# Merge stage: gate and branch products by one level of Strassen's scheme, over halves of the tokens

## The reference

```
proj = h @ w_in                                  # its last 3*1024 columns are the gates
gA, gB, gC = split(sigmoid(gates), 3)
merged = gA * (yA_gated @ w_br_rwkv) + gB * (yB_gated @ w_br_mla) + gC * (yC_gated @ w_br_sb)
x = x + gate * (merged @ w_out)                  # w_out is 1024 x 1024
```

## Time and profile before

| | us |
|---|---|
| median of the runs | 5366.02 |
| profiled execution, first to last instruction | 5380.9 |
| PE busy | 4843.3 (90%) |
| DVE, ACT, POOL busy | 2057.0, 1544.8, 240.7 |
| products of the merge, layer 1 (window 2002 to 2562) | 560, PE busy 559.82 |
| output of the merge, layer 1 (window 2562 to 2690) | 128, PE busy 123.71 |

### The profile page before, as it was taken

The page is one execution under the profiler, slowest core; times in us unless marked ns, Lnnn a source line. Parts: engine busy times, 40 slices in busy tenths (PEclk is TensorE's granted clock), DMA queues, the critical chain, the costliest instruction groups (busy, mean ns, idle before and its releaser), DMA issues. The chain is left out here.

```text
span 5380.9 us, 64260 instructions
## 1 busy us (share of the span) xinstructions
PE 4843.3 (90%) x24624; PEld 3178.1 (59%) x24624; DVE 2057.0 (38%) x4480; ACT 1544.8 (29%) x3518; POOL 240.7 (4%) x506
## 2 busy tenths in 40 slices
PE   6999898788989989999969898987889899899999
PEld 2667567456656655555426676674566566555554
DVE  2355555335534450111123555553355344501111
ACT  2333232235543340000023332322355433400000
POOL 0010100000000000000000101000000000000000
PEclk8999999899999989999979999998999999899999
DMA  5100101210012111211140101012100121112111
GB/s 199 23 12 19 30 9 17 78 48 10 24 43 69 61 54 36 72 59 41 59 155 23 12 19 30 9 17 78 48 10 24 45 69 59 54 36 73 58 41 59
DMA packets 132705, 253.24 MB, mean 47 GB/s; under 512 B 51445, under 2 KB 86517, under 8 KB 126919
## 3 DMA queue, kind: packets, MB, share of 16 engines
q1 hardware_dynamic: 132280, 244.32, 14.3%
q10 hardware_dynamic: 112, 4.72, 0.2%
HBM read 201.66 MB, written 52.06 MB: 47 GB/s over the span
## 5 line engine op out<-in xcount | busy, mean ns | idle before, releaser
L2376 PE MATMUL banks<-hT,w_gate 128*128 128x384 f32 x2304 | 771.4, 488 | 15.9 <-DMA w_branch<-in_w_br 15.9
L2376 PEld LDWEIGHTS banks<-hT,w_gate 128*128 128x128 f32 x2304 | 439.8, 191 | 323.9 <-DMA w_branch<-in_w_br 16.7
L974 PE MATMUL banks<-hT,w_piece 128*128 128x384 f32 x1536 | 564.1, 510 | 9.7 <-ACT raw L1078 9.4
L2143 PE MATMUL banks<-hT,w_piece 128*128 128x384 f32 x1152 | 391.1, 495 | 17.8 <-DMA w_piece<-in_w_cols 16.4
L974 PEld LDWEIGHTS banks<-hT,w_piece 128*128 128x128 f32 x1536 | 288.0, 199 | 186.9 <-issue 27.5
L2380 PE MATMUL banks<-y_branch,w_branch 128*128 128x384 f32 x1152 | 395.1, 486 | 0.0
L2401 ACT ACTIVATE gate_tanh<-banks 128x384 f32<-128x384 f32 x144 | 70.6, 490 | 1065.4 <-PE banks L2380 1065.4
L2143 PEld LDWEIGHTS banks<-hT,w_piece 128*128 128x128 f32 x1152 | 217.0, 193 | 173.8 <-issue 22.1
L2380 PEld LDWEIGHTS banks<-y_branch,w_branch 128*128 128x128 f32 x1152 | 218.9, 190 | 152.6
L2414 DVE SCALAR_TENSOR_TENSOR gate_tanh<-gate_tanh,banks 128x384 f32<-128x384 f32 x96 | 53.2, 554 | 634.1 <-ACT gate_tanh L2401 634.1
L2392 PE MATMUL banks<-w_out,mergedT 128*128 128x512 f32 x576 | 247.5, 592 | 0.0
(11 more groups left out here) (335 smaller groups left out, 8017.9 us busy)
## 6 DMA issues: line engine op xcount, KB each, us to landing
w_piece<-in_w_cols SPq DMA_DIRECT2D x68, 512.0 KB, 4.4
w_ada<-in_w_ada SPq DMA_DIRECT2D x12, 2048.0 KB, 9.5
w_gate<-in_w_cols SPq DMA_DIRECT2D x48, 512.0 KB, 3.4
y_branch<-y_gated SPq DMA_DIRECT2D x18, 768.0 KB, 9.6
w_branch<-in_w_br SPq DMA_DIRECT2D x48, 256.0 KB, 3.5
sb_cached_keysT<-in_sbkT SPq DMA_DIRECT2D x8, 1024.0 KB, 6.7
sb_cached_values<-in_sbv SPq DMA_DIRECT2D x8, 1024.0 KB, 5.1
w_out<-in_w_out SPq DMA_DIRECT2D x16, 512.0 KB, 5.1
```

The costliest lines, as they stand in the source:

```text
L974: last = mm(dst, w[0 if kind in ("k", "v") else 1][:, k, :], hT[:, k, c], start=(k == 0), stop=(k == KD - 1))
L2143: last = mm(ps[:, bank[n], 0:TG], w[wn % 3][:, k, :], hT[:, k, TG * g:TG * g + TG], start=(k == 0), stop=(k == KD - 1))
L2376: nc.tensor.matmul(ps[:, 2 * (u % 4), 0:TG], wg[j % 2][:, k, :], hT[:, k, c], start=(k == 0), stop=(k == KD - 1))
```

## The change

One level of Strassen's scheme, in the form with seven products, is put on both products of the merge. A unit is now (half of the tokens `tp`, branch `b`, pair of output blocks `m`): 2 x 3 x 4 = 24 units per layer. The weights of two output blocks are cut into 2 x 2 parts (output block x half of the contraction), and `hT` or `y_branch` into 2 x 2 parts (half of the contraction x quarter of the tokens, `TQ` = 288). Seven products of parts and of their sums take the place of eight. A product has 4 matmuls for the gate and 2 for the branch, with 288 columns.

The sums of weights (four instructions for the gate, four for the branch in each unit) and of `y_branch` (four for each branch and half of the tokens) are made by GpSimd, those of `hT` by VectorE. Products that several results share are copied out of PSUM by ScalarE (`kept`), and VectorE adds them up (`added`). All weights are loaded twice, once for each half of the tokens. `w_out` goes into `hT`'s space, and x moves in half rows.

The core of the diff (left out: declarations of tiles and semaphores, and the SyncE program, which loads 2 x 512 KB of `w_gate` and 2 x 256 KB of `w_branch` for unit u after product 7 and product 14 of unit u-2):

```diff
+        units = [(tp, b, m) for tp in range(2) for b in range(3) for m in range(KD // 2)]
         @block.gpsimd
+            def combine(w, s, half, sem):
+                a11, a12, a21, a22 = (w[:, i, half * j:half * j + half, :] for i in range(2) for j in range(2))
+                own(G.tensor_tensor(s[:, 0], a21, a22, ALU.add))
+                own(G.tensor_tensor(s[:, 1], s[:, 0], a11, ALU.subtract))
+                own(G.tensor_tensor(a21, a11, a21, ALU.subtract))
+                own(G.tensor_tensor(s[:, 2], a12, s[:, 1], ALU.subtract), sem)
+            for u in range(NU):
+                pool.wait_ge(wg_loaded[u % 2], 32 * (u // 2 + 1))
+                combine(wg[u % 2], wgs[u % 2], KD // 2, gate_sums)
+                if u % PER_Y == 0:
+                    ... four tensor_tensor of 128 x (2 x 288) on Y, then y_sums
+                pool.wait_ge(wb_loaded[u % 2], 32 * (u // 2 + 1))
+                combine(wb[u % 2], wbs[u % 2], HP // 2, branch_sums)
         @block.tensor
-                for k in range(KD):
-                    nc.tensor.matmul(ps[:, 2 * (u % 4), 0:TG], wg[j % 2][:, k, :], hT[:, k, c], ...)
-                for k in range(HP):
-                    last = nc.tensor.matmul(ps[:, 2 * (u % 4) + 1, 0:TG], wb[j % 2][:, k, :], Y[b % 2][:, k, c], ...)
+            def product(bank, w, b, first, last):
+                half = w.shape[1]
+                for k in range(half):
+                    ins = mm(ps[:, bank, 0:TQ], w[:, k, :], b[:, k, :], start=(first and k == 0), stop=(k == half - 1), skip_group_check=True)
+                ins.then_inc(products, 1)
+            for u, (tp, b, m) in enumerate(units):
+                pe.wait_ge(wg_loaded[u % 2], 32 * (u // 2 + 1))
+                if u >= 1:
+                    pe.wait_ge(tanh_done, 4 * u)
+                product(0, w[:, 0, 0:half], hT[:, 0:half, c1], True, False)
+                product(1, w[:, 0, half:KD], hT[:, half:KD, c1], True, True)
+                pe.wait_ge(gate_sums, u + 1)
+                pe.wait_ge(h_sums, tp + 1)
+                pe.wait_ge(kept, 6 * u + 1)
+                product(0, s[:, 1], HS[:, 1], False, False)
+                product(2, s[:, 0], HS[:, 0], True, False)
+                pe.wait_ge(kept, 6 * u + 2)
+                product(0, w[:, 1, 0:half], hT[:, 0:half, c2], False, False)
+                pe.wait_ge(kept, 6 * u + 3)
+                product(2, s[:, 2], hT[:, half:KD, c2], False, True)
+                pe.wait_ge(added, 6 * u + 2)
+                product(0, w[:, 1, half:KD], HS[:, 2], False, True)
+                ... the same seven for the branch: banks 3, 4, 5 for 0, 1, 2, wb and Y for wg and hT,
+                ... waits quarter_read u; branch_sums, y_sums, kept 6u+4; kept 6u+5; kept 6u+6; added 6u+5
         @block.scalar
-                nc.scalar.activation(th[u % 2][:, :], ps[:, 2 * (u % 4), 0:TG], ACT.Tanh, scale=0.5).then_inc(gate_read, 1)
+            for u in range(NU):
+                keep(u, 1, gk[:, 0, :], 0)
+                keep(u, 3, gk[:, 1, :], 0)
+                tanh(u, 0)
+                keep(u, 4, gk[:, 2, :], 2)
+                tanh(u, 1)
+                tanh(u, 2)
+                act.wait_ge(products, 14 * u + 7)
+                if u >= 1:
+                    act.wait_ge(quarter_read, u)
+                do(gq[:, 3, :], ps[:, 0, 0:TQ], ACT.Tanh, scale=0.5).then_inc(tanh_done, 1)
+                keep(u, 8, bk[:, 0, :], 3)
+                keep(u, 10, bk[:, 1, :], 3)
+                keep(u, 11, bk[:, 2, :], 5)
         @block.vector
+            h_sum(0)
+            for u, (tp, b, m) in enumerate(units):
+                add(u, 2, 1, gq[:, 0, :], gk[:, 0, :], 1)
+                add(u, 5, 3, gq[:, 1, :], gk[:, 2, :], 0)
+                add(u, 6, 2, gq[:, 2, :], gk[:, 1, :], 2)
+                if u == NU // 2 - 1:
+                    dve.wait_ge(products, 14 * u + 7)
+                    h_sum(1)
+                add(u, 9, 4, bq[:, 0, :], bk[:, 0, :], 4)
+                quarter(0, 0, 0, bq[:, 0, :])
+                add(u, 12, 6, bq[:, 1, :], bk[:, 2, :], 3)
+                add(u, 13, 5, bq[:, 2, :], bk[:, 1, :], 5)
+                quarter(1, 1, 1, bq[:, 1, :])
+                quarter(2, 0, 1, bq[:, 2, :])
+                quarter(3, 1, 0, ps[:, 3, 0:TQ], quarter_read)
```

More of the change, by code:

```diff
@@ L2356, in _ @@
[L2356 to L2363, removed]
@@ new lines, in _ @@
+            for j in range(4):
+                sp.dma_start(x[j][:, :], x_half(*ups[j])).then_inc(x_moved[j], 16)
+            sp.wait_ge(products, 14 * (NU - 1) + 7)
+            sp.dma_start(w_half(1), A["w_out"][l, :, :, 512:D]).then_inc(w_out_loaded[1], 16)
+            for j, (n, i) in enumerate(ups):
+                sp.wait_ge(updated, 2 * (j + 1))
+                sp.dma_start(x_half(n, i), x[j % 4][:, :]).then_inc(x_moved[j % 4], 16)
+                if j >= 1 and j + 3 < len(ups):
+                    sp.wait_ge(x_moved[(j - 1) % 4], 16 * (2 * ((j - 1) // 4) + 2))
+                    sp.dma_start(x[(j - 1) % 4][:, :], x_half(*ups[j + 3])).then_inc(x_moved[(j - 1) % 4], 16)
@@ new lines, in _ @@
+            banks = (6, 7, 0, 1)
+            pe.wait_ge(merged, NU // 2)
+            for j, (n, i) in enumerate(ups):
+                if i == 0:
+                    pe.wait_ge(w_out_loaded[n], 16)
+                if j == 2:
+                    pe.wait_ge(tanh_done, 4 * NU)
+                if j == 4:
+                    pe.wait_ge(merged, NU)
+                if j >= 4:
+                    pe.wait_ge(update_read, j - 3)
+                for k in range(KD):
+                    last = mm(ps[:, banks[j % 4], :], M[:, k, P * i:P * i + P], w_half(n)[:, k, :], start=(k == 0), stop=(k == KD - 1))
@@ L2396, in _, with keep @@
         def _(act):
[L2397 to L2400, removed]
-                nc.scalar.activation(th[u % 2][:, :], ps[:, 2 * (u % 4), 0:TG], ACT.Tanh, scale=0.5).then_inc(gate_read, 1)
+            do = nc.scalar.activation
+            def keep(u, j, dst, bank):
+                act.wait_ge(products, 14 * u + j)
+                do(dst, ps[:, bank, 0:TQ], ACT.Copy).then_inc(kept, 1)
@@ new lines, in add, with quarter @@
+            def add(u, j, copied, dst, src, bank):
+                dve.wait_ge(products, 14 * u + j)
+                dve.wait_ge(kept, 6 * u + copied)
+                own(V.tensor_tensor(dst, src, ps[:, bank, 0:TQ], ALU.add), added)
+            h_sum(0)
+            for u, (tp, b, m) in enumerate(units):
+                def quarter(q, row, col, src, sem=None):
+                    out = M[:, 2 * m + row, cols(tp, col)]
+                    if b == 0:
+                        own(V.scalar_tensor_tensor(out, gq[:, q, :], 1.0, src, ALU.add, ALU.mult), sem)
+                    else:
+                        own(V.scalar_tensor_tensor(gq[:, q, :], gq[:, q, :], 1.0, src, ALU.add, ALU.mult), sem)
+                        own(V.tensor_tensor(out, out, gq[:, q, :], ALU.add))
+                add(u, 2, 1, gq[:, 0, :], gk[:, 0, :], 1)
[5 more added lines that the diff above has]
+                add(u, 9, 4, bq[:, 0, :], bk[:, 0, :], 4)
+                dve.wait_ge(tanh_done, 4 * u + 1)
+                quarter(0, 0, 0, bq[:, 0, :])
+                add(u, 12, 6, bq[:, 1, :], bk[:, 2, :], 3)
+                add(u, 13, 5, bq[:, 2, :], bk[:, 1, :], 5)
+                dve.wait_ge(tanh_done, 4 * u + 3)
+                quarter(1, 1, 1, bq[:, 1, :])
+                quarter(2, 0, 1, bq[:, 2, :])
+                dve.wait_ge(products, 14 * u + 14)
+                dve.wait_ge(tanh_done, 4 * u + 4)
+                quarter(3, 1, 0, ps[:, 3, 0:TQ], quarter_read)
+                V.engine_nop().then_inc(merged, 1)
@@ L2406, in _ @@
             dve.wait_ge(gate_loaded, 16)
             own(V.tensor_scalar(gate[:, :, :], gate[:, :, :], 0.5, None, ALU.mult))
[L2408 to L2422, removed]
+            put = InOrder(dve, updated)
+            for j, (n, i) in enumerate(ups):
+                dve.wait_ge(updates, j + 1)
+                dve.wait_ge(x_moved[j % 4], 16 * (2 * (j // 4) + 1))
+                put(V.tensor_tensor(t[j % 2][:, :], ps[:, (6, 7, 0, 1)[j % 4], :], gate[:, int(i == NPT), 512 * n:512 * n + 512], ALU.mult))
```

154 lines of the change are left out of this document (101 added, 53 removed).

## The result

The changed kernel takes 5235.05 us (median of 4 runs, 5230.34 to 5236.68) against 5366.52 us for the kernel before: 0.9754 of its time, 95% interval 0.974 to 0.9768. Forecast: 5234, range 5222 to 5288.

What follows compares the result with a forecast made beforehand. TensorE was taken to bound the merge without a gap. Per layer -68.4 + 0.7 + 2.1 - 0.3 = -65.9 us, twice -131.8, took 5366.0 to 5234 us, range 5222 to 5288.

Steps and rivals of the forecast that it cites:

- The likeliest case: Whole kernel: the time comes out as reckoned, 5234 us, own range 5224 to 5262; chance 0.65.
- The stream: Merge products on TensorE: 2016 records of 288 columns at 242.5 ns take 488.9 us, 68.4 us less per layer.
- The narrow waits: Four branch waits per unit on ScalarE copies or VectorE adds: latency of 0.78 to 0.87 us fits in 0.97, cost 0.
- The sums on GpSimd: Weight and y sums: 232 us beside 489 us of TensorE per layer, one unit ahead, hidden behind matmuls, cost 0.
- the second rival: GpSimd slow beside VectorE: if twice as slow, TensorE waits at y sets, about 50 us in all, 5284 us; chance 0.09.
- `h_sum(1)`: VectorE's sums of hT in unit 11 after product 7: TensorE's product 14 stalls, +2.1 us per layer.
- the clock rival: Merge: more gaps lower TensorE's granted clock; half level for a fifth of the stream gives 5430 us; chance 0.03.
- The start: Each layer's first matmul waits for 1.0 MB of gate weights instead of 0.75 MB of both: +0.7 us.
- the output part: Products with w_out after the merge's products: records unchanged; the last store of 256 KB instead of 512 gives -0.3 us per layer.
- The product windows: Sign of being wrong: the merge's two product windows don't shrink to 490 to 495 us each.
- narrow waits don't fit: Each of four branch waits opens a gap of about 0.3 us, 1.2 us a unit, 58 in all: 5292 us; chance 0.17.
- Every product drains: Each of 14 products per unit pays 0.33 us for emptying TensorE's array, 222 us in all: 5456 us; chance 0.06.

Runs made afterwards that it cites:

- before_288: The kernel before, with groups of 288 tokens instead of 384 in the merge's products: 5366.0 us, 0.9998 of the kernel before.
- eighth: The changed kernel with product 9 of each unit run twice: 5288.8 us, 0.9845 of the kernel before.
- copies2: The changed kernel with one extra ScalarE copy ahead of each shared branch product's copy (8, 10, 11): 5248.5 us, 0.9783 of the kernel before.
- copies3: The changed kernel with two extra ScalarE copies ahead of each shared branch product's copy (8, 10, 11): 5275.1 us, 0.9833 of the kernel before.
- pool_gate_half: The changed kernel with GpSimd starting the sums of unit u only when unit u-2 is over: 5231.6 us, 0.9751 of the kernel before.
- early: The changed kernel with products 1 and 2 waiting only for the first 512 KB of gate weights: 5237.2 us, 0.9757 of the kernel before.
- after_again: The changed kernel run again without edits: 5240.7 us, 0.9756 of the kernel before.
- after_3: The changed kernel run a third time without edits: 5236.6 us, 0.9747 of the kernel before.

## Why the prediction was right

The likeliest case happened, 1 us from the forecast. But the terms of the sum come out differently, by 7 us in all, so a hit this close is luck.

- **The stream (-68.4 us a layer)**: right. The records of 288 columns start 243 ns apart, a steady unit takes 20.37 us, and before_288 and eighth show that the number of columns sets it.
- **The narrow waits (0)**: right in effect. No branch wait shows in the steady units, one of 0.20 us in unit 5. The chain itself was sized too short by 0.13 us (TensorE's wake-up 0.12 against 0.05, ScalarE's behind product 8 0.10 against 0.04), so the margin at product 10 is some 0.08 us and not 0.1 to 0.2, and copies2 shows that 0.3 us more of it does cost time.
- **The sums on GpSimd (0)**: right. 235 us busy a layer; the 232 reckoned had 15 us of self-waits in them, so the instructions took 8% longer than reckoned. They are not beside the gate half, as I argued against the second rival; the weights of unit u land right behind product 7 of unit u-2, and POOL works beside the branch half, against VectorE's quarters. The mechanism of that rival is thus there, but it falls on VectorE, which had room, and hardly on POOL: mostly 1.36 us for 512 columns, 1.27 undisturbed (1.23 reckoned), and at most 2.03, in unit 11, beside `h_sum(1)`.
- **`h_sum(1)` (+2.1 us a layer)**: right place, wrong size. It was 3.40 us of idle time and 1.8 more of low clock, 5.2. Two things were missing: quarter 0 takes 0.93 + 1.42 us instead of 0.9 together, beside POOL, and behind the pause 8 or 9 records ran wholly or partly at the lower clock level. The Trainium skill, page "TensorE: Matmul & The Clock Gate", Part 1, says that the clock falls after idle time of TensorE; this pause agrees. The length of the pause alone doesn't decide it: behind 2.44 us (eighth), 2.49 (copies3) and 3.08 (copies2) 6 records took 480 ns too, behind 2.94 us (pool_gate_half, both layers) none; in early they came only 1.3 us behind the pause's end. What decides stays open. Against the clock rival I had written that without idle time above a few us there is no reason for a lower clock; pauses of 2.4 us were enough.
- **The start (+0.7)**: the idle time ahead of the first matmul went from 7.88 and 8.07 us to 9.76 and 9.42 in this trace, but 8.5 to 8.9 in the two repeats: +0.4 to +1.9. The slow records behind it, which the sum has no term for, cost 2.5 and 2.4 us before and 1.8 and 1.7 after.

The merge by the trace: (559.77 + 559.63) - (496.12 + 496.01) = 127.3 us less in the products, 3.2 more at the starts, so 124 us, or 125 with the output part, which is 0.6 us shorter in layer 2 (128.54 for 129.10; I had 0.3 a layer). The forecast said 131.8, and the medians moved by 131.5. The terms that were mis-sized are the stall (5.2 for 2.1 us a layer) and in this trace the start. The product windows came out at 496 us and not at 490 to 495 because of the 3.1 us more of the stall and the 1.8 us of slow records at the start.

The 7 us between the trace and the medians lie outside the products, and I can't assign them. The other stages spread that much: the first product of layer 1 starts anywhere from 1991.9 to 2008.3 us in runs that have had the same work up to there, and the profiled execution of the kernel before was 14.9 us above its median, as I carried over, the one after at its median. But spread alone is not shown to be the reason, since after_again and after_3 against the kernel before beside them moved by 129.1 and 135.7 us, more than 125 both times.

Rivals: *narrow waits don't fit* priced 1.2 us a unit; a steady unit shows nothing, and even with 0.31 us more in each of three copies (copies2) it was 0.32. *Every product drains*: no step between products is longer than within one. *The clock*: 0.99 over the products, and no slow record but at the start and behind the pause.

## What to carry to other kernels

A stage in which TensorE has no idle time pays for fewer columns at full price, and records can be narrowed to 288 columns of f32 at a price of 2.5 ns for each record; count columns, then check by a chain of latencies from rows that each product between two dependent ones is longer than copy plus wake-ups. Work that is moved to idle engines costs where it meets a block: look for the longest run of instructions that stands in one engine's queue ahead of something TensorE waits for, and cut it up. A pause of TensorE must be priced with the slow records behind it.

## What was not expected of the hardware

- A VectorE instruction with two SBUF operands, 0.46 us alone, took 1.40 to 1.41 us beside GpSimd's elementwise instructions of 1.36 us, while one with an operand in PSUM kept its 0.45 us.
- Behind a pause of 3.40 us 6 records took 480 ns instead of 242.5 and 2 or 3 something between, 1.8 us in all; 6 did so behind pauses of 2.44, 2.49 and 3.08 us in other runs, and behind one of 2.94 us not one did.
- TensorE's weight load followed ScalarE's end by 0.12 us in this kernel, and by 0.05 in the row used for the forecast.
- Once in each layer, in unit 5 (unit 4 in copies2, nowhere in copies3), ScalarE began a copy 0.28 us later than in the units beside it.
